# Spreading the loads of the last rows, and finishing the last pair in quarters behind an fp32 expert product

## The reference

```python
h2 = rmsnorm(x, norm2_g) * (1 + sc2) + sh2
x = x + g2 * peer(h2.reshape(B * T, D), w_pq, sub_keys, u_tab, v_tab).reshape(B, T, D)
# inside peer, for each row t: eidx (8 heads x 16 picks), g = softmax of their scores
u = jnp.take(u_tab, eidx, axis=0)
vv = jnp.take(v_tab, eidx, axis=0)
act = jax.nn.gelu(jnp.einsum('td,ted->te', hb, u).astype(jnp.float32))
return jnp.einsum('te,ted->td', (g * act).astype(hb.dtype), vv)
# and at the very end
y_prompt = rmsnorm(xp, final_g)
y_sample = rmsnorm(xs, final_g)
```

## Time and profile before

| | us |
|---|---|
| median of 3 executions (3979.19 to 4003.27) | 3989.54 |
| the profiled execution | 4007.67 |
| its span, first to last instruction | 4005.9 |
| TensorE busy | 3664.2 |
| VectorE busy | 2663.2 |
| GpSimd busy | 1093.2 |
| ScalarE busy | 444.6 |

### The profile page before, as it was taken

The page is one execution under the profiler, slowest core; times in us unless marked ns, Lnnn a source line. Parts: engine busy times, 40 slices in busy tenths (PEclk is TensorE's granted clock), DMA queues, the critical chain, the costliest instruction groups (busy, mean ns, idle before and its releaser), DMA issues.

```text
span 4005.9 us, 34359 instructions
## 1 busy us (share of the span) xinstructions
PE 3664.2 (91%) x12423; PEld 1946.2 (49%) x12423; DVE 2663.2 (66%) x4400; ACT 444.6 (11%) x962; POOL 1093.2 (27%) x865
## 2 busy tenths in 40 slices
PE   4899999997995789799989999999988899996997
PEld 1566545466552664355734444444464344442443
DVE  1258852148788885888976767777698666564763
ACT  2100004110000350111600000000051000000000
POOL 1000001106444553454232222222234322221420
PEclk7999997898998689899999999999999999998998
DMA  9877753359999999999699999999979999999994
GB/s 367 270 236 256 255 192 124 130 190 390 410 414 415 360 368 346 389 388 379 238 410 420 420 410 422 422 421 416 390 283 371 417 421 421 422 421 388 420 421 177
DMA packets 348592, 1402.88 MB, mean 350 GB/s; under 512 B 25584, under 2 KB 150472, under 8 KB 207333
## 3 DMA queue, kind: packets, MB, share of 16 engines
q0 software_dynamic: 117056, 832.57, 51.8%
q1 hardware_dynamic: 230368, 563.29, 37.7%
q10 hardware_dynamic: 1008, 4.98, 0.3%
HBM read 1375.24 MB, written 31.55 MB: 351 GB/s over the span
## 4 chain that ended last, share of the span: by engine, by line
PE 53%; DMA 31%; issue 9%; DVE 4%; POOL 2%; another core or an unknown queue 1%; ACT 0%; SPq 0%; DVEq 0%; POOLq 0%; ACTq 0%
DMA R<-in_u_experts,MS 25%; PE bank L1281 21%; PE bank L859 8%; PE bank L887 7%; PE bank L1074 4%; PE bank L1081 4%; DMA R<-in_w_ada 3%; DMA R<-in_v_experts 2%; POOL R L740 2%; PE bank L799 1%; PE bank L1248 1%; PE bank L776 1%; DVE R L2019 1%; PE bank L1136 1%
## 5 line engine op out<-in xcount | busy, mean ns | idle before, releaser
L740 POOL DMA_INDIRECT R<-in_u_experts,MS x640 | 896.2, 1400 | 1629.5 <-DVE MS L2101 1362.7
L2101 DVE CUSTOM_DVE_ANT_0 R<-R 128x2048 f32<-128x2048 f32 x374 | 857.8, 2294 | 390.3 <-DMA R<-in_u_experts,MS 368.8
L1281 PE MATMUL bank<-R,RB 128*128 128x512 f32 x2304 | 1020.7, 601 | 82.4 <-DMA R<-in_v_experts 82.3
L1281 PE MATMUL bank<-RB 128*128 128x512 f32 x1792 | 778.2, 592 | 0.0
L1281 PEld LDWEIGHTS bank<-R,RB 128*128 128x128 f32 x2304 | 441.7, 193 | 651.4 <-issue 554.1
L2101 DVE CUSTOM_DVE_ANT_0 R<-R,RB 128x2048 f32<-128x2048 f32 x266 | 608.7, 2289 | 113.4 <-DMA R<-in_u_experts,MS 112.3
L1281 PEld LDWEIGHTS bank<-RB 128*128 128x128 f32 x1792 | 340.5, 190 | 428.6 <-issue 428.6
L2216 DVE SCALAR_TENSOR_TENSOR R<-R,MS 128x2048 f32<-128x2048 f32 x128 | 301.4, 2355 | 199.1 <-DMA R<-in_v_experts,MS 198.6
L859 PE MATMUL bank<-RB,R 128*128 128x256 f32 (+1 forms) x1536 | 400.2, 421 | 24.5 <-DMA R<-in_w_pq 21.3
L859 PEld LDWEIGHTS bank<-RB,R 128*128 128x128 f32 x1536 | 294.3, 193 | 123.3 <-DMA R<-in_w_pq 21.9
L1074 PE MATMUL bank<-RB,R 128*128 128x384 f32 x1024 | 335.5, 489 | 1.2 <-ACT RB L1438 0.7
(11 more groups left out here) (352 smaller groups left out, 2248.4 us busy)
## 6 DMA issues: line engine op xcount, KB each, us to landing
R<-in_v_experts SPq DMA_DIRECT2D x144, 1024.0 KB
RB<-in_v_experts SPq DMA_DIRECT2D x112, 1024.0 KB, 9.2
R<-in_w_ada SPq DMA_DIRECT2D x48, 2048.0 KB, 13.6
R<-in_w_in SPq DMA_DIRECT2D x20, 2048.0 KB, 16.9
R<-in_w_in SPq DMA_DIRECT2D x24, 1024.0 KB, 25.8
R<-in_w_out SPq DMA_DIRECT2D x8, 2048.0 KB, 8.1
R<-in_w_pq SPq DMA_DIRECT2D x8, 2048.0 KB
R<-in_w_out SPq DMA_DIRECT2D x16, 1024.0 KB, 14.5
```

The lines of the kernel that those rows point to most:

```text
L740: pool.indirect_dma_start(dst, None, table, bass.IndirectOffsetOnAxis(ap=expert[T_ % 2][:, c:c + 1], axis=0)).then_inc(signal, 16)
L1281: x = pe.matmul(PB[4 * h + q][:, :], W[:, i, h * P:(h + 1) * P], vring[slot][:, q * PW:(q + 1) * PW], start=(i == 0), stop=(i == NKEY - 1))
L2101: V.tensor_tensor_reduce(u, u, x, 1.0, 0.0, ALU.mult, ALU.add, dots[t % 2][:, h * TOPK + s:h * TOPK + s + 1]).then_inc(dots_done, 1)
```

## The change

The 8 MiB of `finals()` are no longer issued in one piece behind V block 84. Eight groups of 1 MiB stand one each behind the V blocks 28, 36, 44, ... 84 of the second pair. In `last_rows` the sample tile is finished, with its output row, before the pair is touched. TensorE gives a signal for each of the 8 products of the last V block in place of one for the block, and VectorE takes each bank on its own signal, adds the residual quarter at once, and ScalarE squares that quarter. The first tile is scaled and written after five quarters; the second tile's output is written and stored in two halves.

```diff
+        part_out = dots[1][:, 0:8]
...
-            def finals():
-                sp.dma_start(g2b, rows(mod_d, [[0, P]], D, 5 * D)).then_inc(s_fin, 16)
-                sp.dma_start(fgb, rows(ins["final_g"].tensor, [[0, P]], D)).then_inc(s_fin, 16)
-                for i in range(2):
-                    sp.dma_start(x1r[i], x1_d[i]).then_inc(s_fin, 16)
-                    sp.dma_start(accd[i], acc_d[i]).then_inc(s_fin, 16)
-                sp.dma_start(x1r[2], x1_d[TP]).then_inc(s_fin2, 16)
-                for b in range(NB):
-                    sp.dma_start(g2s[NS * b:NS * b + NS],
-                                 rows(mod_d, [[0, NS]], D, (1 + b) * 6 * D + 5 * D)).then_inc(s_fin2, 16)
+            def final_rows(r):
+                if r == 2:
+                    sp.dma_start(g2b, rows(mod_d, [[0, P]], D, 5 * D)).then_inc(s_fin, 16)
+                elif r == 3:
+                    sp.dma_start(fgb, rows(ins["final_g"].tensor, [[0, P]], D)).then_inc(s_fin, 16)
+                elif r == 4:
+                    for b in range(NB):
+                        sp.dma_start(g2s[NS * b:NS * b + NS],
+                                     rows(mod_d, [[0, NS]], D, (1 + b) * 6 * D + 5 * D)).then_inc(s_fin2, 16)
+                elif r < 7:
+                    sp.dma_start(x1r[r - 5], x1_d[r - 5]).then_inc(s_fin, 16)
+                elif r == 7:
+                    sp.dma_start(x1r[2], x1_d[TP]).then_inc(s_fin2, 16)
+                else:
+                    sp.dma_start(accd[r - 8], acc_d[r - 8]).then_inc(s_fin, 16)
...
-                    if pair == 1 and i == 84:
-                        finals()
+                    if pair == 1 and 28 <= i <= 84 and i % 8 == 4:
+                        final_rows(i // 8 - 1)
...
             for i in range(2):
-                sp.wait_ge(s_y, 4 + i)
-                sp.dma_start(yp[2 + i], x1r[i]).then_inc(s_yst, 16)
+                for o in range(1 + i):
+                    at = slice(o * 2 * PW, (o + 1) * 2 * PW if i else D)
+                    sp.wait_ge(s_y, 4 + i + o)
+                    sp.dma_start(yp[2 + i][:, at], x1r[i][:, at]).then_inc(s_yst, 16)
...
-                    x.then_inc(vp_used, 1)
+                            if pair == 1 and i == NKEY - 1:
+                                x.then_inc(vp_used, 1)
+                    if pair == 0 or i < NKEY - 1:
+                        x.then_inc(vp_used, 1)
...
-            last_squares(0, x1r[2], acc, 10)
-            last_squares(1, x1r[0], accd[0], 0)
-            last_squares(2, x1r[1], accd[1], 1)
+            last_squares(0, x1r[2], acc, fin[:, 10:11])
             row_sqrt(1, 10, 1)
-            row_sqrt(2, 0, 2)
+            for n in range(8):
+                h, at = n // 4, slice(n % 4 * PW, (n % 4 + 1) * PW)
+                last_squares(1 + n, x1r[h][:, at], accd[h][:, at], part_out[:, n:n + 1])
+                if n == 4:
+                    row_sqrt(2, 0, 1)
+            row_sqrt(3, 5, 1)
...
-                dve.wait_ge(vp_used, NKEY * 2)
-                dve.wait_ge(s_x1l, 32)
-                for h in range(2):
-                    for q in range(4):
-                        at = slice(q * PW, (q + 1) * PW)
-                        ch.mark(TT(accd[h][:, at], PB[4 * h + q][:, :], g2b[:, at], ALU.mult))
-                    ch.sync()
-                    TT(x1r[h], x1r[h], accd[h], ALU.add).then_inc(f_x, 1)
                 dve.wait_ge(s_sq, 2 * T + 1)
                 row_scale(1, 10, 1)
                 row_out(x1r[2], 13)
-                dve.wait_ge(s_sq, 2 * T + 3)
-                row_scale(2, 0, 2)
-                for h in range(2):
-                    row_out(x1r[h], 6 + h)
+                dve.wait_ge(s_x1l, 32)
+
+                def last_quarter(n):
+                    h, at = n // 4, slice(n % 4 * PW, (n % 4 + 1) * PW)
+                    dve.wait_ge(vp_used, NKEY * 2 + n)
+                    ch.link(TT(accd[h][:, at], PB[n][:, :], g2b[:, at], ALU.mult))
+                    TT(x1r[h][:, at], x1r[h][:, at], accd[h][:, at], ALU.add).then_inc(f_x, 1)
+
+                def last_scale(h):
+                    dve.wait_ge(s_sq, 2 * T + 1 + 4 * (h + 1))
+                    ch.link(V.tensor_reduce(fin[:, 5 * h:5 * h + 1], part_out[:, 4 * h:4 * h + 4], AX.X, ALU.add))
+                    row_scale(2 + h, 5 * h, 1)
+
+                for n in range(5):
+                    last_quarter(n)
+                last_scale(0)
+                row_out(x1r[0], 3)
+                for n in range(5, 8):
+                    last_quarter(n)
+                last_scale(1)
+                for o in range(2):
+                    row_out(x1r[1], 8, slice(o * 2 * PW, (o + 1) * 2 * PW))
```

More of the change, by code:

```diff
@@ L626, in _ @@
             for i in range(2):
-                sp.wait_ge(s_y, 4 + i)
-                sp.dma_start(yp[2 + i], x1r[i]).then_inc(s_yst, 16)
-            sp.wait_ge(s_yst, 16 * T)
+                for o in range(1 + i):
+                    at = slice(o * 2 * PW, (o + 1) * 2 * PW if i else D)
+                    sp.wait_ge(s_y, 4 + i + o)
+                    sp.dma_start(yp[2 + i][:, at], x1r[i][:, at]).then_inc(s_yst, 16)
+            sp.wait_ge(s_yst, 16 * (T + 1))
         @block.gpsimd
@@ L1588, in row_sqrt, with last_squares @@
                 A(fin[:, at + 2 * w:at + 3 * w], fin[:, at + w:at + 2 * w], ACT.Sqrt).then_inc(f_r, 1)
-            def last_squares(n, x, junk, at):
+            def last_squares(n, x, junk, sum_out):
                 act.wait_ge(f_x, n + 1)
-                A(junk, x, ACT.Square, accum_out=fin[:, at:at + 1]).then_inc(s_sq, 1)
+                A(junk, x, ACT.Square, accum_out=sum_out).then_inc(s_sq, 1)
             gate_exp(1)
@@ L2029, in row_scale, with row_out @@
                 ch.link(refine(fin[:, at + 3 * w:at + 4 * w], fin[:, at + w:at + 2 * w], fin[:, at + 4 * w:at + 5 * w]))
-            def row_out(x, at):
-                STT(out=x, in0=x, scalar=fin[:, at:at + 1], in1=fgb, op0=ALU.mult, op1=ALU.mult).then_inc(s_y, 1)
+            def row_out(x, at, cols=slice(0, D)):
+                STT(out=x[:, cols], in0=x[:, cols], scalar=fin[:, at:at + 1], in1=fgb[:, cols],
+                    op0=ALU.mult, op1=ALU.mult).then_inc(s_y, 1)
             def first_pair_out(k):
```

## The result

The changed kernel took 3947.07, 3943.98 and 3954.74 us, median 3947.07 against 3989.54; the ratio is 0.991, 95% interval 0.9884 to 0.9936. Beside the kernel before on one chip, in more runs, it was 0.9922 (0.9896 to 0.9948, 11 runs against 22), which is 31 us of 3989.54 (21 to 41). The forecast was 3958 with 3942 to 3978, and 31.9 us less. The two medians of three executions differ by 42.5 us; the ratio from more runs is the better measure of the gain.

The account below looks back on a forecast made before the run. Bound: TensorE's second dense product, with a 37.25 us hole waiting for V blocks; DMA engines full. VectorE free at 3950.9 + 20.0 + 3.1 = 3974.0 in place of 4005.9, 31.9 less; median forecast 3958, range 3942 to 3978.

Parts of the forecast that it names:

- The hole: TensorE's wait for a V block behind block 84 in the second dense product: 37.3 us, forecast to go.
- the restart: The first V block after TensorE's wait takes 8.78 us instead of 7.03: 1.75 us, forecast to go.
- 3.0 us at block 45: TensorE stall at V block 45, behind the eight small loads: 3.0 us, bounds 0 and 5.
- A single 1 MiB in front makes it 15 at most: A V block with one 1 MiB load ahead in SP's queue lands within 15 us; it is needed in 20.6.
- The gathers pay: Sample gathers sharing the full DMA pipe: 9.2 MiB more pass before the last pick, landing it 22.9 us later.
- The new bound: VectorE after the last pick: 10.5 us to the first bank, 20.0 to the last output row, 3.1 for the store.
- The gathers matter: Opposite rival, gathers don't matter: last pick in by 3927.7, end 44.6 us less, median 3945; chance 0.15.
- the stall was not spread: Opposite rival, stall only spread: each of eight groups holds its next V block 4.7 us, median 3979; chance 0.14.
- the chain that grew out of the sample tile: Rival: everything after the last pick becomes the end, last pick 82 us late, median 4017; chance 0.05.
- the second edit: New last rows, sample tile ahead of the pair, then quarters: quarters bring 1.0 us, half-tile store takes 3.1.
- The last pick stays before 3925: Sign that the forecast is wrong; the last pick was expected added 20 to 27 us later than 3917.5.

Follow-up runs that it names:

- loads only: Kernel before with only the eight load groups spread, its old last rows kept; ratio to the kernel before 0.9897.
- halved: Changed kernel with V blocks 88 to 127 of the second pair loaded in half their columns; ratio to the kernel before 0.9875.
- pair first: Changed kernel with the quarters directly behind the sample tile's additions, its scale behind the fourth quarter; ratio to the kernel before 0.9903.
- rows behind: The pair first kernel with the last two tiles' residual rows loaded when pick 127 is added, first pair's stores behind; ratio to the kernel before 0.9911.
- loads in twos: Changed kernel with the eight groups two by two behind V blocks 36, 52, 68 and 84; ratio to the kernel before 0.9896.
- the two with other small loads: Changed kernel with the eight small loads reading sixteen distinct rows each, or made one load; 33.5 us from last pick to end in both.

## Why the prediction was right

**The hole.** 37.3 and 1.75 for the restart were forecast to go; they went. The 3.0 us at block 45 were the term that was a little large: the waits there were 0 and 1.97 us in the two profiles of the changed kernel, and 1.64 (loads only), 1.47 (halved), 0.34 (pair first) and 3.86 (rows behind) in the others. In the changed kernel's first profile the eight loads were through 12.4 us after block 44 and not 15.7, so block 45 landed 20.1 us after its issue, 0.3 before its product began. In the second profile they took 15.0, and block 45 landed 22.5 after its issue. So the first profile's zero is partly luck, and the bounds of 0 to 5 were right. "A single 1 MiB in front makes it 15 at most" held: 12.2 and 12.5 us for the two blocks that were read. The holes behind groups of two, four and eight grow with what is queued: no hole for two plain MiB, 5.8 with the small loads among them, 6.6 for four, 16.9 for four with the small loads, 37 for all eight.

**The gathers pay.** The forecast counted 9.2 MiB at 2.49 us, 22.9; counted from block 17 the last pick came 20.6 later in one profile and 24.0 in the other. The half-block kernel had the last pick 48 us earlier against the product's end. That 20 MiB at 2.49 are 50 is in part luck: with that pick so early, the last V blocks and the stores also fell behind it. The run shows what paces the picks, not the price of a MiB.

**The new bound.** From the last pick to the first bank 10.5 us were forecast and 10.50 measured; from the first bank to the last output row 20.0 and 19.8; the store 3.1 and 3.2. The five profiles that have the changed tail and are bound by the pick (the changed kernel twice, loads in twos, and the two with other small loads) have 33.5 us from the pick to the end, for 33.6.

**The rivals.** The gathers matter (the pick is what the end follows); the stall was not spread (no hole in the first profile, 0 to 4 us at one place in others); and the chain that grew out of the sample tile is at the front of the end, but 20 us late and not 80.

**What the forecast had wrong.** It credited the second edit with 1.0 us and a shorter store. Taken against the old end it costs 3.2 us in this place, as loads only shows. The new order waits 4.2 us for ScalarE in five places (2.07, 0.79, 0.63 and twice 0.33), the old one 2.4 (2.10 and 0.33). Four quarters of 1.32 do in 5.3 us what took 4.7, for each of two tiles. One more scale and two sums of parts add some 1.5, and the half-tile store gives 1.4 back. The forecast's own rows said so: the old order behind a last pick at 3940.4 would have ended at 3940.4 + 4.7 + 21.0 + 4.6 = 3970.7, ahead of its 3974.0. The sum came out because it was made for the whole end and not as a difference of edits.

**A sign that has to be read with care.** "The last pick stays before 3925" was to show the forecast wrong, and on the trace's own clock the last pick is at 3911.8, before 3925 and even before the 3917.5 of the kernel before. That clock runs from the start of the span, and the changed kernel reached block 17 26.3 us earlier for reasons outside the change. From block 17 the mark is 759.5, which is 3938.1 on the clock of the profile before, for 3940.4. The sign should have been given from a common mark.

**Luck in the median.** The medians of the changed kernel (3947.07, then 3952.11) are 6 to 11 us under 3958. From block 17 the span gained 34.3 for 31.9, so some 2 us of that are the change's; the rest is within the spread between executions.

## What to carry to other kernels

When a pipe is full, work out who gives the bytes: a stall taken off one chain makes the other one late by the bytes that now pass earlier (here 9.2 MiB by the forecast's count, 21 to 24 us), and the new time is set by whichever chain is then last, not by the old time less the stall. What a ring of blocks can bear in front of a block is its lead less the usual landing time, so small groups cost TensorE next to nothing (0 to 3.9 us, and only behind the eight small loads), and one burst costs nearly all of it (37 us). Look again at the last stage's order after such an edit: the new last rows, with the side tile finished first, gained 8.6 us while that tile was early and lost 3.2 once it was late.

## What the hardware showed that was not expected

Executions that run the same code up to the second product reach it 20 us apart among the changed kernels, and up to 30 us with the kernel before's, which is more than most of the effects told here. From the last pick to the end the time is steady to 0.1 us where the code is the same (33.5 five times). From block 17 to the product's end the two profiles of the changed kernel agree to 0.6 us, and from block 17 to the last pick only to 3.4. While the eight loads of 16 rows of 8 KB passed, all transfers together moved 225 to 273 GB/s in the changed kernel's first profile and 183 to 216 in its second, with the DMA share at 1.0; beside loads of 128 rows it is 421. Neither distinct rows nor a single transfer for all eight brought the rate back. Two stores of 1 MiB took 18.6 us beside gathers and 11.05 without.
